# A table of constants multiplied into a free PSUM bank in the short stages of a two-layer decoder step

## What is computed

```
layer 0:  x = rms_norm(h)
          q, kc, vc, ks, vs, kw, vw, gates, u = split(x @ w_in)
          per-head RMS norm of q and of the keys
          NSA: three branches (compressed, selected, window), softmax with a relative-position bias,
               mixed by the gates; the selected blocks are the 16 best by the compressed branch
          S5:  diagonal complex state space over u, gelu, then out = z * sigmoid(z @ w_glu + b)
          h += concat(nsa, s5) @ w_out
layer 1:  q, k, v = split(rms_norm(h) @ w_in); sliding-window attention (128) with a sink per head
          h += attention @ w_out
each:     h += (gelu(causal_conv3(x @ w_up)) * (x @ w_gate)) @ w_down,  x = rms_norm(h)
```

## Time and profile before

| | |
|---|---|
| median of 3 runs | 3202.26 us (3201.84 to 3204.47) |
| the profiled execution | 3207.11 us |
| its span, first to last instruction | 3205.3 us |
| mean granted clock of TensorE | 0.939 |
| busy share of TensorE, VectorE, ScalarE, GpSimd | 92%, 45%, 29%, 23% |

### The profile page before, as it was taken

One profiled execution on the slowest core, in us unless ns is written; L12 is line 12 of the kernel. 1 busy time (PEld: TensorE's weight loads), 2 busy tenths in 40 slices (PEclk: granted clock), 3 DMA queues, 4 the chain that ended last, 5 costly groups with the idle time before them and its releaser, 6 DMA issues. The chain is left out here.

```text
span 3205.3 us, 51177 instructions
## 1 busy us (share of the span) xinstructions
PE 2954.8 (92%) x19701; PEld 2833.1 (88%) x19701; DVE 1442.0 (45%) x3259; ACT 944.4 (29%) x1692; POOL 742.1 (23%) x526
## 2 busy tenths in 40 slices
PE   7988996759999799999999999989789999999998
PEld 6987886449998499999999999968689999999998
DVE  4517773446776344431442443157644441441441
ACT  4213444335554132110211123047432110210211
POOL 1124552002111132221221224232132222221221
PEclk9998998757999899999999999979889999999999
DMA  6223552032000521111111111110021111111112
GB/s 175 80 86 114 158 158 63 1 71 108 2 1 23 242 63 40 46 46 46 46 48 44 52 42 44 41 42 1 14 63 34 52 46 46 46 46 46 46 48 72
DMA packets 270117, 195.93 MB, mean 61 GB/s; under 512 B 56388, under 2 KB 260286, under 8 KB 263407
## 3 DMA queue, kind: packets, MB, share of 16 engines
q1 hardware_dynamic: 262859, 143.19, 15.7%
q0 software_dynamic: 6912, 50.33, 4.4%
q10 hardware_dynamic: 184, 0.20, 0.0%
HBM read 176.64 MB, written 24.42 MB: 63 GB/s over the span
## 5 line engine op out<-in xcount | busy, mean ns | idle before, releaser
L590 PE MATMUL ps<-xf_hi,w_hi 128*128 128x344 f32 x2352 | 757.8, 322 | 9.9 <-POOL w_lo L581 9.9
L592 PE MATMUL ps<-xf_hi,w_lo 128*128 128x344 f32 x2352 | 754.3, 321 | 0.0
L591 PE MATMUL ps<-xf_lo,w_hi 128*128 128x344 f32 x2352 | 753.6, 320 | 0.0
L581 POOL TENSOR_TENSOR w_lo<-w_raw,w_hi 128x1024 fp32r<-128x1024 f32 (+1 forms) x162 | 384.9, 2376 | 1471.9 <-ACT w_hi L577 1471.9
L590 PEld LDWEIGHTS ps<-xf_hi,w_hi 128*128 128x128 f32 x2352 | 444.0, 189 | 11.3 <-issue 11.2
L591 PEld LDWEIGHTS ps<-xf_lo,w_hi 128*128 128x128 f32 x2352 | 443.9, 189 | 0.7 <-issue 0.7
L592 PEld LDWEIGHTS ps<-xf_hi,w_lo 128*128 128x128 f32 x2352 | 444.1, 189 | 0.0
L590 PE MATMUL ps<-hid_hi,w_hi 128*128 128x344 f32 x1056 | 339.8, 322 | 0.0
L592 PE MATMUL ps<-hid_hi,w_lo 128*128 128x344 f32 x1056 | 338.0, 320 | 0.0
L591 PE MATMUL ps<-hid_lo,w_hi 128*128 128x344 f32 x1056 | 337.3, 319 | 0.0
L577 ACT CAST w_hi<-w_raw 128x1024 fp32r<-128x1024 f32 (+1 forms) x162 | 165.6, 1022 | 388.8 <-PE ps L592 384.0
(11 more groups left out here) (565 smaller groups left out, 5381.8 us busy)
## 6 DMA issues: line engine op xcount, KB each, us to landing
w_raw<-in_ffn_w_up_dram SPq DMA_DIRECT2D x44, 512.0 KB, 3.7
w_raw<-in_ffn_w_gate_dram SPq DMA_DIRECT2D x44, 512.0 KB
w_raw<-in_ffn_w_down_dram SPq DMA_DIRECT2D x32, 448.0 KB, 3.5
w_raw<-in_ffn_w_down_dram SPq DMA_DIRECT2D x16, 512.0 KB, 3.6
w_raw<-in_a_w_in_dram SPq DMA_DIRECT2D x14, 512.0 KB, 3.8
w_raw<-in_c_w_in_dram SPq DMA_DIRECT2D x10, 512.0 KB, 3.9
residual<-hT SPq DMA_DIRECT2D x1, 4128.0 KB
hT<-residual SPq DMA_DIRECT2D x1, 4128.0 KB, 17.3
```

Of the source, the lines that this page charges most:

```text
L581: pool.tensor_tensor(self.parts.lo[:, slot, 0:kt, :], self.raw[:, slot, 0:kt, :], self.parts.hi[:, slot, 0:kt, :].bitcast(F32), ALU.subtra ...
L590: pe.matmul(psum, w_hi, x_hi, start=(a == 0), stop=False)
L591: pe.matmul(psum, w_hi, x_lo, start=False, stop=False)
L592: ins = pe.matmul(psum, w_lo, x_hi, start=False, stop=(a == kt - 1))
```

## The change

A helper multiplies 64 rows of the unit matrix with the table `b_win` into a bank that holds nothing at that time; nobody reads the result. It waits for no semaphore and sends none. One call with `count` is that many matmuls of 512 columns.

```diff
+def keep_busy(k, pe, count, bank):
+    for _ in range(count):
+        pe.matmul(k.ps[:, bank, :], k.ident[0:64, :], k.b_win[:, :], start=True, stop=True)
```

Four of the calls in the diff, the others are alike:

```diff
@@ stage_split
+        @block.tensor
+        def _(pe):
+            keep_busy(k, pe, 4, 7)
+
@@ stage_dense
             pe.sem_inc(ring.s_prod, CREDIT)
             pe.sem_inc(s_free, CREDIT)
+            keep_busy(k, pe, 5, 7)
@@ stage_attend
             @block.tensor
             def _(pe):
+                keep_busy(k, pe, 1 if swa else 4, 7)
                 for t in range(n_steps):
@@ stage_s5_compress
                     if name in ("Q0", "Q1", "Q2", "Q3"):
+                        if n == 0:
+                            keep_busy(k, pe, 8, 6)
                         pe.wait_ge(s_v, 2 * q + x // 2 + 1)
```

More of the change, by code:

```diff
@@ L1047, in _ @@
                               stop=True).then_inc(s_sum, 1)
+                keep_busy(k, pe, 1, 7)
             @block.vector
@@ L1417, in keys_transposed @@
         pe.transpose(k.ps[0:NB, 1, P:2 * P], self.kvT[:, 0, T:TA], k.ident[:, :]).then_inc(self.s_ktr, 1)
+        keep_busy(k, pe, 3, 0)
     def vector_first(self, dve):
@@ L1907, in _ @@
             def _(pe):
+                keep_busy(k, pe, 5, 5)
                 pe.wait_ge(s_in, 32)
@@ L1917, in _ @@
                 ins.then_inc(s_sc, 1)
+                keep_busy(k, pe, 2, 5)
                 pe.wait_ge(s_dve, 7)
@@ L2661, in _ @@
                 pe.transpose(k.ps[0:NB, 0, 192:216], gT[:, T:TA], k.ident[0:24, 0:24]).then_inc(s_tr, 1)
+                keep_busy(k, pe, 3, 1)
             @block.vector
@@ L2703, in tensor @@
         k, w2, hid = self.k, self.w2, self.hid
+        keep_busy(k, pe, 5, 6)
         pe.wait_ge(self.s_w, 16 * len(self.loads))
@@ L2829, in _ @@
                 ins.then_inc(s_qk, 1)
+                keep_busy(k, pe, 1, 5)
                 for n, src in enumerate((sc, pr)):
@@ L2953, in _ @@
             def _(pe):
+                keep_busy(k, pe, 4, 5)
                 pe.wait_ge(s_b, 1)
                 pe.transpose(k.ps[0:16, 0, 0:64], base[:, :], k.ident[0:64, 0:64]).then_inc(s_t, 1)
+                keep_busy(k, pe, 3, 5)
                 pe.wait_ge(s_tc, 1)
@@ L3076, in _ @@
                 scores(NB - 1)
+                keep_busy(k, pe, 5, 0)
                 pe.wait_ge(s_p, 1)
```

## The result

The changed kernel takes 3208.46 us in the median of 11 runs (3204.58 to 3222.01), before 3201.84 (3196.8 to 3206.36): a ratio of 1.0027 with an interval of 1.0017 to 1.0037. It is slower, by little more than a measurement can tell, as forecast (3209). The profiled execution has a span of 3209.9 us.

What follows compares the result with a forecast made beforehand. TensorE, busy 92% of the span, was taken to bound the kernel, through its queued work and its clock. Costs 9.5 less gains 2.7 give 6.8 us on the median 3202.26: forecast 3209, its own range 3202 to 3213, overall 3193 to 3216.

Steps and rivals of the forecast that it cites:

- Price of a call: Each constant multiply on TensorE: 0.86 us warm, 1.71 cold, plus 0.25 once per series for draining; 64 rows save nothing.
- No rise of the clock with 64 rows: Cold sites: a full TensorE with 64-row operands stays at half clock, read from L2709, busy 13.60 of 13.70 us at 0.50.
- Costs, 9.5: Delays by calls outlasting their waits, from stage_split to the dense stage of layer 1: 9.5 us, bounds 4 and 13.
- dense in layer 0: stage_dense, layer 0: 5 cold calls end at 1130.2, where the transposes began at 1129.42; cost 0.8 us.
- the second series of the window samples: swa_sample: the 2 calls after the scores hide in the softmax only until 2318.45 and reach 2319.07; cost 0.6 us.
- the NSA start: NSA attention opening: 4 cold calls delay the first score by 1.8 us, 0.6 covered by a transfer; cost 1.2 us.
- the window attention with its keys: keys_transposed, 3 calls, 1.2 us; SWA attention start, 1 call ahead of its first score, 1.7 us.
- Hidden calls at nothing: Calls in S5 compress, CompressPrompt, cmp_sample, sample_caches and others fit into idle time: no cost taken, some at-most cases.
- Gains, 2.7: Later clock fall at warm sites: CompressPrompt 0.6 (up to 6.96), sample_caches 0.7, cmp_sample 0.6, two head norms 0.4 each.
- Rival 1: The calls raise the clock, so attention openings, L2709 and dense openings run warm: 33 us gained, 3169; chance 0.13.
- Rival 2: Nothing measurable: delays fall into next-stage waits, the late clock fall returns the rest; net 0 to 3, 3203; chance 0.13.
- Rival 3: A later attention start costs one more half-clock stretch before the clock rises: 6.5 us more, 3216; chance 0.08.

Runs made afterwards that it cites:

- e9: Against the kernel before: only 4 calls of 64 rows ahead of the third task's scores in the NSA attention; 3204.41 us, ratio 1.0006.
- e7: Against the kernel before: only 4 calls of 128 rows ahead of the third task's scores in the NSA attention; 3200.13 us, ratio 0.9990.
- e2: The change with only the 64-row calls that the prediction had at nothing; 3200.14 us, ratio 0.9997 to the kernel before.
- e4: Against the kernel before: only the 8 calls of 64 rows ahead of the first Q0 of stage_s5_compress; 3205.69 us, ratio 1.0005.
- e6: The change with 128 rows, some calls dropped (S5, attention starts, others), three counts fitted, e7's series added; 3177.66 us, ratio 0.9927 to before.
- e3: The change with only the 64-row calls that the prediction charged; 3208.86 us, ratio 1.0021 to the kernel before.
- e10: e7 with one more 128-row call ahead of every fourth task of the first two tiles; 3196.40 us, ratio 0.9978 to before.

## Why the prediction was right

- **Price of a call:** right, 7.16 us for 4 cold calls against 7.09, and 64 rows save nothing. (What it calls 128-column records in its last paragraph are these, of 512 columns.)
- **No rise of the clock with 64 rows:** right. 10.20 us of constant multiplies at 0.50 in the change, and e9 against e7, are the direct evidence; L2709, on which the step rested, was the right row to ask. Two things stay open. The 128-row calls also have other constants, and no run changes one without the other; L2709, whose 64 rows hold other numbers again, speaks for the rows. And the prediction passed over a row of its own: the NSA opening, with operands of 128 rows, fills 51.17 of 51.20 us and stays at 0.50, so 128 rows in a TensorE that looks full are not always enough.
- **Costs, 9.5:** right in place, a fifth too small: the ten charged steps came to 11.7 in two profiles. The terms that were mis-sized are dense in layer 0 (0.8, measured 1.14), the second series of the window samples (0.6, 1.06), the NSA start (1.2, 1.59) and the window attention with its keys (2.9, 3.37): the 0.25 for draining, which they left out, comes in at direct successors too (in the dense stage the next matmul starts 8.80 after the first call, reckoned 8.53), and at the window samples the idle time was read to begin 0.14 early.
- **Hidden calls at nothing:** right by e2 (0.9997) and e4 (1.0005).
- **Gains, 2.7:** not shown. L2709 gave nothing (13.92 again, the term had 0.6), for the reason that kept the term small: the calls end before the wait does. The bound of 6.96 was the right size for what is there: 128-row calls fitted to the wait took 6.5 of it in e6. The 1.8 at the compressed samples is in e2 and e3, which share no call there, so it is not assigned.
- **Net, 6.8:** measured 6.6. That the two agree so closely owes something to luck: a cost too small by 2.2 met returns that the runs don't place.
- **Rival 1** (the calls raise the clock) falls for 64 rows, and of its price of 33 us the 128 rows with fitted counts gave most: e6 is 26 under its before. **Rival 2** (delays absorbed) falls by e3. **Rival 3** (a later rise in the attention) did not happen; the rise moved within 745 to 770 in all kernels with a cold opening, also in those without calls there.

## What to carry to other kernels

Here, filling a waiting TensorE paid with operands on all 128 rows (0.9950); on half of them it cost its full time and left a cold clock cold (1.0027). A series belongs where it ends just as the real work can start: a cold call too many delays that work by 1.7 us, and a wait of 2.30 us behind a 64-row series, or of 2.65 us behind a 128-row one, gave away all or nearly all of the gain at L2709 (13.92 and 12.76 us). In the sparse first tiles of the attention the clock fell back unless a call came now and then; whether that pays in time, beyond the series alone, was not shown. And a clock that rises behind a new call proves little by itself: look whether it also rises there in a run without the call.

## What the runs showed of the hardware

Raising and holding are different: 64-row work ran 13.6 us back to back at 0.50 without a rise, and the same 128 records ran 7.40 us at full clock when it was up as they began. At the S5 block the clock, once up, fell after 3.4 us without work and stayed up for 10.2 us with 64-row calls in the first 6.7 of them (e7 and e2). In the sparse first tiles of the attention the clock fell after 13.5 us in e7 and stayed up through 47.5 us in e10, with one more call (0.86 us at full clock) per four tasks. One profile against another can differ by 8 us in a stretch that the change does not touch (the NSA row of the table), through the moment at which the clock rises; a second kernel without the suspected part is what shows it.
